# A fourth weight chunk split ahead of the residual pair's work in the down projection of a two-layer decoder step

## What is computed

```python
for l in range(DEPTH):                                   # DEPTH = 2, D_MODEL = 2048
    xn = _rmsnorm(hp, norm_mix[l])
    ...                                                   # attention and retention, w_in, w_o
    hp = _mix_out(hp, o_swa, o_ret, g_r, w_o[l])
    hp = _ffn(hp, norm_ffn[l], w_gate_up[l], w_down[l])   # D_FF = 5632
def _ffn(x, g, w_gate_up, w_down):
    xn = _rmsnorm(x, g)
    a, b = jnp.split(jnp.einsum('btd,df->btf', xn, w_gate_up), 2, axis=-1)
    return x + jnp.einsum('btf,fd->btd', jax.nn.silu(a) * b, w_down)
y_prompt = _rmsnorm(hp, norm_final)
```

## Time and profile before

| | |
|---|---|
| runs (us) | 2784.89, 2784.15, 2774.39 |
| median (us) | 2784.15 |
| span of the profiled execution (us) | 2771.3 |
| that execution's own time | the page gives none; its span is 12.85 us under the median, 3.09 us under the lowest run |
| PE busy | 2692.2 us, 97% of the span |
| DVE / ACT / POOL busy | 1498.9 / 1247.4 / 175.6 us |
| HBM traffic | 167 GB/s over the span |

### The profile page before, as it was taken

One profiled execution on the slowest core, in us unless ns is written; L12 is line 12 of the kernel. 1 busy time (PEld: TensorE's weight loads), 2 busy tenths in 40 slices (PEclk: granted clock), 3 DMA queues, 4 the chain that ended last, 5 costly groups with the idle time before them and its releaser, 6 DMA issues.

```text
span 2771.3 us, 54196 instructions
## 1 busy us (share of the span) xinstructions
PE 2692.2 (97%) x19946; PEld 2666.1 (96%) x19946; DVE 1498.9 (54%) x2371; ACT 1247.4 (45%) x2229; POOL 175.6 (6%) x219
## 2 busy tenths in 40 slices
PE   5899999999999999999999999999999999999997
PEld 5899999999999999999999999999999999999997
DVE  5346656655555555445455655566555555545445
ACT  3345554544444444444444544445444444444443
POOL 3400001100000000000020000010000000000000
PEclk8999999999999999999999989999999999999998
DMA  6836655555555555555555545555555555555554
GB/s 162 255 110 186 190 182 163 161 167 164 162 162 171 162 164 166 155 157 158 159 168 184 176 147 168 158 182 167 161 166 166 166 160 167 166 160 157 156 161 136
DMA packets 425972, 458.96 MB, mean 166 GB/s; under 512 B 16317, under 2 KB 414989, under 8 KB 425840
## 3 DMA queue, kind: packets, MB, share of 16 engines
q1 hardware_dynamic: 407488, 404.38, 47.7%
q0 software_dynamic: 14432, 48.36, 6.0%
q10 hardware_dynamic: 3984, 5.32, 0.5%
HBM read 434.53 MB, written 27.53 MB: 167 GB/s over the span
## 4 chain that ended last, share of the span: by engine, by line
PE 63%; issue 30%; DMA 2%; DVE 2%; DVEq 1%; POOLq 1%; ACT 1%; ACTq 0%; SPq 0%
PE ps L966 20%; PE ps L970 19%; PE ps L968 19%; DMA raw<-w_in 2%; PE ps L1128 1%; DVE w_lo L642 1%; DVE xg_lo L654 1%; PE ps L1206 1%; PE ps L1215 1%; PE ps L1167 0%; PE ps L985 0%; PE ps L1144 0%; PE ps L1196 0%; DVEq L895 0%; POOLq L1290 0%
## 5 line engine op out<-in xcount | busy, mean ns | idle before, releaser
L642 DVE TENSOR_TENSOR w_lo<-raw,w_hi 128x512 fp32r<-128x512 f32 x1572 | 1076.8, 694 | 961.1 <-ACT w_hi L358 944.9
L358 ACT ACTIVATE w_hi<-raw 128x512 fp32r<-128x512 f32 x1572 | 959.4, 620 | 1201.8 <-PE ps L970 1155.4
L966 PE MATMUL ps<-xg_hi,w_hi 128*128 128x288 f32 x4224 | 1287.7, 305 | 37.4 <-DVE w_lo L642 33.1
L968 PE MATMUL ps<-xg_lo,w_hi 128*128 128x288 f32 x4224 | 1257.9, 298 | 0.0
L970 PE MATMUL ps<-xg_hi,w_lo 128*128 128x288 f32 x4224 | 1257.2, 298 | 0.0
L966 PEld LDWEIGHTS ps<-xg_hi,w_hi 128*128 128x128 f32 x4224 | 803.8, 190 | 44.7 <-DVE w_lo L642 32.5
L968 PEld LDWEIGHTS ps<-xg_lo,w_hi 128*128 128x128 f32 x4224 | 805.0, 191 | 0.5
L970 PEld LDWEIGHTS ps<-xg_hi,w_lo 128*128 128x128 f32 x4224 | 803.2, 190 | 0.0
L966 PE MATMUL ps<-cat_hi,w_hi 128*128 128x288 f32 x1024 | 304.4, 297 | 15.4 <-DVE w_lo L642 15.4
L970 PE MATMUL ps<-cat_hi,w_lo 128*128 128x288 f32 x1024 | 303.0, 296 | 0.0
L968 PE MATMUL ps<-cat_lo,w_hi 128*128 128x288 f32 x1024 | 303.0, 296 | 0.0
(11 more groups left out here) (196 smaller groups left out, 1378.4 us busy)
## 6 DMA issues: line engine op xcount, KB each, us to landing
raw<-w_gate_up SPq DMA_DIRECT2D x352, 512.0 KB, 3.6
raw<-w_in SPq DMA_DIRECT2D x178, 512.0 KB, 3.8
raw<-w_down SPq DMA_DIRECT2D x160, 512.0 KB, 3.7
raw<-w_o SPq DMA_DIRECT2D x64, 512.0 KB, 4.4
st<-state POOLq DMA_DIRECT2D x16, 1024.0 KB, 9.3
new_rs<-st POOLq DMA_DIRECT2D x16, 1024.0 KB, 7.0
raw<-w_down SPq DMA_DIRECT2D x32, 256.0 KB, 2.9
yT<-x_res ACTq DMA_DIRECT2D x4, 576.0 KB, 3.1
```

The costliest lines, as they stand in the source:

```text
L358: nc.scalar.activation(w_hi[q][:, 0:n, :], raw[s][:, n * (j % 2):n * (j % 2) + n, :], ACT.Copy).then_inc(hi_ready[q], 1)
L642: nc.vector.tensor_tensor(w_lo[q][:, 0:n, :], raw[s][:, n * (j % 2):n * (j % 2) + n, :], w_hi[q][:, 0:n, :].bitcast(F32), ALU.subtract).th ...
L966: nc.tensor.matmul(out, w_hi[q][:, t, cols], x_hi[:, x, :], start=(k == 0), stop=False, skip_group_check=True)
L968: nc.tensor.matmul(out, w_hi[q][:, t, cols], x_lo[:, x, :], start=False, stop=False, skip_group_check=True)
```

## The change

The down projection alone is changed. On both engines chunk 3 of its first round is split ahead of the loop. Within the loop ACT splits four chunks of the following round instead of three ahead of its wait for `x_new`; DVE splits three, adds the pair to the residual, splits the fourth, and then makes the pair's low parts. ACT squares the pair first and makes its high parts second. For this `lo_of_pair` is taken out of `add_to_residual`; in the output projection (`R_O`) the order stays as it was. PE, POOL and SP have the same program.

```diff
--- before.py
+++ after.py
@@ -613,17 +613,18 @@
                 with act.Fori(0, (FT - KT) // 2) as i:
                     gate_up(i + KT // 2, hid_hi[:, bass.ds(i * 2, 2), :])
 
+                split(r0 + R_DOWN, LEAD, LEAD + 1)
                 with act.Fori(0, 4) as i:
                     for c in range(2):
                         r = r0 + R_DOWN + i * 6 + 3 * c
-                        split(r, LEAD, 8)
+                        split(r, LEAD + 1, 8)
                         split(r + 1, 0, 8)
                         split(r + 2, 0, 8, DOWN_ROUNDS[2])
-                        split(r + 3, 0, LEAD)
+                        split(r + 3, 0, LEAD + 1)
                         n = layer * 16 + 8 + i * 2 + c
                         act.wait_ge(x_new, n + 1)
-                        residual_pair(i * 4 + 2 * c, layer * 2 + 2, n + 8)
-                split(r0 + ROUNDS, LEAD, LEAD + 1)
+                        pair_squares(i * 4 + 2 * c, n + 8)
+                        pair_hi(i * 4 + 2 * c, layer * 2 + 2)
             rms("rms_mix", DEPTH)
             for i in range(4):
                 act.wait_ge(y_ready, 4 * i + 4)
@@ -888,17 +889,17 @@
                                             cat_hi[:, bass.ds(g * 2 + HEADS, 2), :].bitcast(F32),
                                             ALU.subtract).then_inc(cat_ready, 1)
 
-                def add_to_residual(a, r, i, c, n, norm):
+                def add_to_residual(a, r, i, c):
                     multiplied(dve, r)
                     xs = x_res[:, bass.ds(i * 4 + 2 * c, 2), :]
                     nc.vector.tensor_tensor(xs, acc[a], xs, ALU.add).then_inc(acc_read[a], 1)
                     dve.drain().then_inc(x_new, 1)
-                    lo_of_pair(i * 4 + 2 * c, norm, n)
 
                 with dve.Fori(0, 4) as i:
                     for c in range(2):
                         split_on(r0 + R_O + i * 2 + c, GLEAD)
-                        add_to_residual(c, r0 + R_O + i * 2 + c, i, c, layer * 16 + i * 2 + c + 8, layer * 2 + 1)
+                        add_to_residual(c, r0 + R_O + i * 2 + c, i, c)
+                        lo_of_pair(i * 4 + 2 * c, layer * 2 + 1, layer * 16 + i * 2 + c + 8)
 
                 split_on(r0 + R_FFN, GLEAD)
                 reciprocal_std("rms_ffn", layer)
@@ -927,15 +928,17 @@
                 with dve.Fori(0, (FT - KT) // 2) as i:
                     gate_up(i + KT // 2, hid_hi[:, bass.ds(i * 2, 2), :], hid_lo[:, bass.ds(i * 2, 2), :])
 
+                split(r0 + R_DOWN, LEAD, LEAD + 1)
                 with dve.Fori(0, 4) as i:
                     for c in range(2):
                         r = r0 + R_DOWN + i * 6 + 3 * c
-                        split(r, LEAD, 8)
+                        split(r, LEAD + 1, 8)
                         split(r + 1, 0, 8)
                         split(r + 2, 0, 8, DOWN_ROUNDS[2])
                         split(r + 3, 0, LEAD)
-                        add_to_residual(c, r + 2, i, c, layer * 16 + 8 + i * 2 + c + 8, layer * 2 + 2)
-                split(r0 + ROUNDS, LEAD, LEAD + 1)
+                        add_to_residual(c, r + 2, i, c)
+                        split(r + 3, LEAD, LEAD + 1)
+                        lo_of_pair(i * 4 + 2 * c, layer * 2 + 2, layer * 16 + 8 + i * 2 + c + 8)
 
 
             reciprocal_std("rms_mix", DEPTH)
```

## The result

| | before | after |
|---|---|---|
| median of six runs (us) | 2781.77 | 2755.77 |
| lowest to highest (us) | 2774.39 to 2784.89 | 2750.16 to 2768.97 |
| span of the profiled execution (us) | 2771.3 | 2748.6 |
| its own time (us) | not given | 2750.16 |

The six runs of the kernel before are the three of its page and three more. The ratio is 0.9924, with a 95% interval of 0.990 to 0.9948: 0.76% faster, or 21 us (14 to 28); the medians themselves are 26.0 us apart. The prediction was 2764.6 us, in a range from 2754 to 2773, and 19.6 us or 0.7% less than before. The measured median is 8.8 us under it and 1.8 us above the lower end of the range.

A forecast was written before the change was run, and what follows sets the result against it. PE was taken to bound the kernel, losing time to 14 down-projection gaps waiting for DVE. Closing them (18.7 us) plus 0.9 at the end takes 19.6 from 2784.15: 2764.6 us, range 2754 to 2773.

The forecast's parts named there:

- What bounds: PE, busy 97% of the span, loses time in the down projections to 14 gaps, 1.27 or 1.39 us each, awaiting DVE.
- Part 1: Between pairs in the down projection, chunk 3 split first is ready by 1180.45 against 1182.64 wanted, with no instruction added.
- Part 2: Chunk 4, next to be late between pairs, still comes 0.43 us early, 0.29 behind `c` = 0, so costs nothing.
- rival of a short wait for chunk 4: Between pairs a new wait of PE for chunk 4 leaves 0.5 us per gap: 2771.6 us; chance 0.17.
- Part 3: Squares before high parts on ACT start the closing chain of squares, POOL and PE's sum earlier, saving 0.86 us at program end.
- The sum: Gaps of both layers' down projections, 18.7 us, and 0.9 at the end: 19.6 us off, to 2764.6 us.
- The step from a span to a median: For the whole program, the median of the runs was taken to stay 12.85 us above the profiled span.

The follow-up runs named there:

- fourth experiment: The kernel before with chunk 3 split ahead of the pair on ACT alone, DVE's order untouched: ratio 0.9991.
- two last experiments: The changed kernel with one, then two, spare low-part instructions on DVE ahead of the pair's low parts: ratios 0.9916 and 0.9937.
- last experiment: The changed kernel with two spare low-part instructions (0.86 us) on DVE ahead of the pair's low parts: ratio 0.9937.
- third experiment: The changed kernel with ACT's high parts ahead of the squares again, chunk 3 still early: ratio 0.9924 to the kernel before.
- first experiment: The kernel before with POOL adding squares in the down projection only once DVE has made chunk 3's low part: ratio 0.9952.

## Why the prediction was right

- **What bounds.** Right. 14 gaps worth 18.7 us were counted, and with the wait at the end the sum was 19.6 us, which is what the trace of the changed kernel gives back (last table). By the end of the first layer's down projection the changed kernel is 18.7 us ahead in the two traces (PE resumes at 1382.23 instead of 1400.95), but 9.5 of this it had at the first addition of the program (449.3 against 458.8), ahead of any change; the down projection gave 9.2, half of 18.7. The second gives as much, and the wait at the end of the program 0.95.
- **Part 1.** Right: chunk 3 is ready 2.5 us early, and the same move on ACT alone changes nothing (fourth experiment), so it is DVE's part of it that counts.
- **Part 2.** Right in sign, low in size. The slack had been put at 0.43 and, behind `c` = 0, 0.29; the trace shows 0.56 behind both, and the two last experiments put it at 0.65. Three terms were off. ACT starts 0.33 us behind the end of DVE's addition (1168.43 to 1168.76), where 0.41 (1179.33 to 1179.74) had been carried over from a start with `pair_hi` first. The low part beside POOL was given a length, 1.10 us from its own start, and so a later start behind `c` = 0 was charged with 0.14. In the trace it is its end that is fixed, 0.31 us behind the end of POOL's addition, and a later start costs nothing. And PE's start behind chunk 4 was put at 0.15 us, where the last experiment shows 0.05. All three made the slack look smaller than it is, so the rival of a short wait for chunk 4 was further off than its chance of 0.17 says.
- **Part 3.** PE's sum starts 3.68 us behind the start of the last addition instead of 4.63, so 0.95 us against 0.86 predicted, and the third experiment, without this part, waits 1.0 us longer there.
- **The sum against the result.** 19.6 us were predicted; at equal clock the runs say 20.3, the ratio says 21, the traces differ by 22.7 and the medians by 26.0. The forecast of the time itself, 2764.6 us, was 8.8 us too high: 2.4 because the median of the kernel before fell from 2784.15 to 2781.77 us with three more runs, 6.4 because the medians moved by more than the change is worth. The clocks that a few runs happen to get, at 2.5 us for each 0.001, can do that, but those of the six runs before are not on record, so it isn't shown. That the median stayed inside the range, by 1.8 us, is luck. The step from a span to a median (12.85 us, left as it was) does not carry over either: it is 7.2 us in the changed kernel, whose profiled execution was the fastest of its six.

  The 3 us by which the traces differ too much lie in stages whose program is the same. Stretches ahead of the change, before and then after (columns as in the earlier trace rows):

```profile
0.00:460.00 460.00, 420.28 (x3009) 408.34 (x3010) 249.23 (x454) 209.45 (x432) 77.82 (x102) 0.95 0.60 179
```

```profile
0.00:460.00 460.00, 423.15 (x3080) 411.40 (x3081) 255.22 (x463) 215.03 (x442) 79.84 (x104) 0.97 0.60 182
```

71 matmuls more are the 9.5 us: PE is busy for 2.9 us more, and the other 6.6 go with a clock of 0.97 instead of 0.95. In the second layer's attention stage it goes the other way:

```profile
1518.80:1778.80 260.00, 259.83 (x1871) 252.47 (x1870) 142.38 (x288) 124.37 (x270) 19.14 (x24) 0.95 0.53 165
```

```profile
1500.00:1760.00 260.00, 259.83 (x1818) 252.50 (x1816) 140.21 (x283) 123.20 (x268) 19.14 (x24) 0.92 0.52 163
```

Here the changed kernel (second row) is the slower, by 53 matmuls with PE busy as long, and by its first addition of the second layer (1800.91 against 1813.33) its lead of 18.7 us is down to 12.4. So the granted clock in the attention stages, where it isn't at its full level all the time, is most of what separates these two traces outside of the change, and it separates whole runs too (spans of 2748.6 us at 0.984 and 2767.4 at 0.978 for the changed kernel). What sets it was not looked for.
- **What was not seen.** The prediction named POOL's two additions beside DVE's long instructions and yet told the gap as one of order, and its sum would have come out the same with either. The first experiment shows that 1.12 of 1.33 us went away with POOL's additions alone. The change wins because it lays the chain, POOL's delay included, where 0.56 us or more are to spare, not because it takes the delay out.

## What to carry to other kernels

Before a chain is reordered, look at whether one of its instructions is longer than its line's median, and who runs beside it: moving the neighbour may give most of the gain. Price what is late next in the same terms as what is late now, and read the result from a distance that repeats in the trace (here, one addition to the next), since whole runs scatter by more than such a change is worth. Where whole runs have to be compared, set each beside its mean granted clock: here that alone brought the standard deviation of the runs from 7.2 us down to 1.7. When two engines pass a chunk on, moving it on one of them is worth nothing if it waits in the other's queue.

## What the runs showed of the hardware

An instruction of DVE with two inputs in SBUF and an addition on POOL hinder each other, and both can pay. DVE's low part took 0.94 to 1.14 us instead of 0.52 and its chunk 1.28 to 1.30 instead of 0.69. Whatever their start, from 0.02 us ahead of POOL's addition to 0.17 behind it for the low part and from 0.09 to 0.44 behind it for the chunk, the low part ended 0.31 us and the chunk 0.55 us behind the end of the addition. So the time of such an instruction is told by POOL's end and not by a length of its own. Whether it waits all that time, with a part of its shown duration outside the wait, or works beside POOL at a lower pace, is not shown. The other way round POOL's additions took 0.89 us instead of 0.81 when a low part had begun 0.3 us ahead of them (before, behind `c` = 0), and 1.20 and 1.07 when DVE's splits ran one behind the other (first experiment).

PE standing still for some 1 us at a time did not lower its granted clock: it reads 1.00 in the first layer's down projection with its 7 gaps, and 1.00 in the second layer's too, from 2480 to 2750 us.
